# Block three first in the mixer's output, woven TensorE work ahead of its row pair, a third norm buffer

## The reference

```python
x = x + g1 * (mixed @ w_out)                 # the mixer's output
h = modulate(rms_norm(x, norm2_g), sh2, sc2)
q = (h @ w_query).reshape(B, T, 8, 2, 128)   # peer_ffn
s = einsum('bthpd,hpkd->bthpk', q, sub_keys)
s_top, i_top = top_k(s, 16)                  # then top 16 of the 16 x 16 pair sums
idx, gate = chosen experts, softmax(best_s)  # 128 of each for a token
act = gelu(einsum('td,ted->te', h, down[idx]))
y = einsum('te,ted->td', act * gate, up[idx])
# two layers on x and ctx: pooling mixer, then attention; each followed by
x = x + g2 * (silu(a) * v) @ w_down          # a, v from a depthwise conv of h @ w_up
```

## Time and profile before

| | us |
|---|---|
| median of 3 runs | 3761.59 (3760.1 to 3765.12) |
| the profiled execution | 3768.46 |
| its span | 3766.4 |

### The profile page before, as it was taken

The page is one execution under the profiler, slowest core; times in us unless marked ns, Lnnn a source line. Parts: engine busy times, 40 slices in busy tenths (PEclk is TensorE's granted clock), DMA queues, the critical chain, the costliest instruction groups (busy, mean ns, idle before and its releaser), DMA issues.

```text
span 3766.4 us, 59546 instructions
## 1 busy us (share of the span) xinstructions
PE 3306.8 (88%) x24177; PEld 1947.6 (52%) x24177; DVE 2408.0 (64%) x4781; ACT 1114.4 (30%) x2905; POOL 1014.9 (27%) x1021
## 2 busy tenths in 40 slices
PE   7998899899998876666567999999999998999998
PEld 4556666788876332222122333333368854468853
DVE  3865635687756766588777787764444147457765
ACT  2442212444422332333334344332222023410000
POOL 1024410345420333333342233323200000034432
PEclk8999999999999999777788999999999999999999
DMA  4147630000024999999999999989834421012233
GB/s 184 45 184 264 226 113 23 2 11 3 3 86 145 383 414 417 415 405 415 403 414 373 357 389 375 375 344 388 333 108 145 132 74 43 1 68 90 90 123 145
DMA packets 146412, 800.88 MB, mean 213 GB/s; under 512 B 13934, under 2 KB 33773, under 8 KB 62812
## 3 DMA queue, kind: packets, MB, share of 16 engines
q0 software_dynamic: 76048, 543.64, 36.1%
q1 hardware_dynamic: 68940, 251.34, 18.3%
q10 hardware_dynamic: 1152, 2.10, 0.1%
HBM read 794.92 MB, written 2.10 MB: 212 GB/s over the span
## 4 chain that ended last, share of the span: by engine, by line
PE 54%; DVE 13%; DMA 10%; ACT 4%; issue 2%; POOL 0%; DVEq 0%; POOLq 0%; ACTq 0%
PE bank L104 19%; PE bank L2721 8%; DMA row<-in_experts,idxs 7%; PE bank L3154 7%; PE bank L3170 4%; PE bank L4244 3%; DVE row L2914 3%; DMA wring<-in_experts,idxs 2%; PE bank L3946 2%; PE bank L2668 1%; PE bank L1108 1%; DVE wring L2914 1%; PE bank L1089 1%; PE bank L1880 1%; ACT cf L2811 1%
## 5 line engine op out<-in xcount | busy, mean ns | idle before, releaser
L2721 PE MATMUL bank<-row,dg 64*64 64x512 f32 x2920 | 431.8, 703 | 212.2 <-ACT dg L2817 211.8
L2914 DVE CUSTOM_DVE_ANT_0 row<-row,bank 128x1024 f32<-128x1024 f32 x365 | 445.6, 1221 | 192.4 <-DMA row<-in_experts,idxs 154.7
L2981 POOL DMA_INDIRECT row<-in_experts,idxs x365 | 362.3, 993 | 712.7 <-PE bank L2721 643.5
L2721 PEld LDWEIGHTS bank<-row,dg 64*64 64x64 f32 x2920 | 114.9, 148 | 470.6 <-issue 470.0
L3154 PE MATMUL bank<-s_hid,wring 128*128 128x512 f32 x704 | 327.3, 610 | 0.0
L104 PE MATMUL bank<-hT,wring 128*128 128x256 f32 (+1 forms) x864 | 286.6, 492 | 3.0 <-ACT sq L898 3.0
L2808 ACT ACTIVATE act<-dots 128x2 f32<-128x2 f32 x256 | 51.8, 203 | 710.6 <-DVE dots L2914 710.2
L2721 PE MATMUL bank<-wring,dg 64*64 64x512 f32 x1176 | 180.1, 708 | 91.0 <-ACT dg L2817 90.9
L2981 POOL DMA_INDIRECT wring<-in_experts,idxs x147 | 141.7, 964 | 368.7 <-PE bank L2721 264.3
L3154 PEld LDWEIGHTS bank<-s_hid,wring 128*128 128x128 f32 x704 | 129.0, 192 | 200.1 <-issue 199.3
L2914 DVE CUSTOM_DVE_ANT_0 wring<-wring,bank 128x1024 f32<-128x1024 f32 x147 | 179.5, 1221 | 81.0 <-DMA wring<-in_experts,idxs 67.5
(11 more groups left out here) (731 smaller groups left out, 6376.5 us busy)
## 6 DMA issues: line engine op xcount, KB each, us to landing
wring<-in_ffn_up SPq DMA_DIRECT2D x66, 1024.0 KB, 6.8
wring<-in_ada_w SPq DMA_DIRECT2D x64, 1024.0 KB, 6.6
wring<-in_ffn_down SPq DMA_DIRECT2D x32, 704.0 KB, 4.3
wring<-in_ffn_w_down SPq DMA_DIRECT2D x20, 1024.0 KB, 6.5
wring<-in_w_in SPq DMA_DIRECT2D x7, 2048.0 KB, 8.2
wring<-in_peer_w_query SPq DMA_DIRECT2D x8, 1024.0 KB, 25.6
wring<-in_attn_w_qkv SPq DMA_DIRECT2D x3, 2048.0 KB, 7.8
row<-in_experts,idxs POOLq DMA_INDIRECT x365, 9.9
```

Source lines behind the costliest of these rows:

```text
L2721: ins = pe.e.matmul(self.ks[t][64 * half:64 * half + 64, :], self.dg[u % 4][p, 0:64], row[p, 1024 + half * 512:1536 + half * 512], start=( ...
L2914: e.tensor_tensor_reduce(row, row, P.pairs[0], 1.0, 0.0, MUL, ADD, self.dots[:, g % 2, x:x + 1]).then_inc(*V.up("pg_dot", j))
L2981: e.indirect_dma_start(self.places[r], None, P.i["experts"], bass.IndirectOffsetOnAxis(ap=idu[:, b, j % 128:j % 128 + 1], axis=0)).then_in ...
```

## The change

- `MixerOut`: on PE, only block 3's first half is transposed at first; the gates of blocks 2 and 1 come ahead of the output products; an output product is cut in two parts of four matmuls (`part` 0 reads only the delta-rule half), and both first parts of block 3 run before both second parts. Ahead of block 3's row transposes stands only the first part of one product of block 2 (before, both whole products). The other outputs follow after the scores. On DVE the mean step of the norm becomes a function of its own, and two additions of block 2 move behind the first eight steps of `choose`. ACT is ordered to match.
- `Experts`: the query tiles 0 to 7 get four places instead of two (a spent part of the constants, and the scan's `y`), and another order of loads. The fourth gather waits for tile 7 instead of tile 6.
- `Experts.pe`: the woven work of steps u-1 and u runs ahead of the row products of the pair.
- `n10` gets three buffers; only unit 1 stands ahead of the transposes, and turn u-2 follows unit u.
- The loads of the rotation table and of the gains stay at the start of `Qkv`'s stage; the diff doesn't change them.

```diff
-        self.n10 = HiddenState(self, 1, 0, "ffn0", "n10", "ffn0_down_x", 0, [5, 2, 3, 4])
+        self.n10 = HiddenState(self, 1, 0, "ffn0", "n10", "ffn0_down_x", 0, [5, 2, 3, 4], 3)
...
+        self.mean(dv, 3)
         self.normed(dv, 3)
         self.heads_dv(dv, 0)
+        choice, f = P.experts.choose(dv, 3, 0), self.first
+        for _ in range(8):
+            next(choice)
         self.added(dv, 2, 0)
+        next(choice)
         self.added(dv, 2, 1)
-        choice, f = P.experts.choose(dv, 3, 0), self.first
-        for _ in range(11):
+        for _ in range(2):
             next(choice)
         self.added(dv, 1, f)
...
+        self.mean(dv, 2)
         self.added(dv, 1, 1 - f)
         self.added(dv, 0, 1 - f)
-        for b in (2, 1, 0):
+        self.normed(dv, 2)
+        for b in (1, 0):
+            self.mean(dv, b)
+        for b in (1, 0):
             self.normed(dv, b)
...
         x = P.experts
-        for b in self.BLOCKS:
-            self.turned_ac(ac, b, 0)
-        self.root_ac(ac, 2)
+        self.turned_ac(ac, 3, 0)
         ac.wait_ge(*P.at("ro_bonus", 0))
         self.turned_ac(ac, 3, 1)
+        self.root_ac(ac, 2)
         self.root_ac(ac, 1)
+        for b in (2, 1, 0):
+            self.turned_ac(ac, b, 0)
         self.turned_ac(ac, 2, 1)
+        self.squares(ac, 3)
+        self.root(ac, 3)
         for q in range(4):
...
         self.gate_pe(pe, 3)
-        for b in self.BLOCKS:
-            self.turn_pe(pe, b, 0, P.ogdn[:, b])
+        self.turn_pe(pe, 3, 0, P.ogdn[:, 3])
         self.gate_pe(pe, 2)
+        self.gate_pe(pe, 1)
...
         self.heads_pe(pe, 3)
-        self.out_pe(pe, ws, 3, 0)
-        self.out_pe(pe, ws, 3, 1)
-        self.gate_pe(pe, 1)
+        for part in range(2):
+            for half in range(2):
+                self.out_pe(pe, ws, 3, half, part)
+        P.cycle((6, 7, 0, 3, 6, 7, 0, 6, 3, 7, 1))
+        for b in (2, 1, 0):
+            self.turn_pe(pe, b, 0, P.ogdn[:, b])
         self.heads_pe(pe, 2)
...
-        self.out_pe(pe, ws, 2, 0)
         self.heads_pe(pe, 1)
         self.gate_pe(pe, 0)
-        self.out_pe(pe, ws, 2, 1)
+        self.out_pe(pe, ws, 2, 0, 0)
         P.cycle((2, 3, 4, 5))
         self.rows_pe(pe, 3)
...
-        self.out_pe(pe, ws, 1, f)
-        self.out_pe(pe, ws, 0, f)
+        self.out_pe(pe, ws, 2, 0, 1)
+        for b, half in ((2, 1), (1, f), (0, f)):
+            for part in range(2):
+                self.out_pe(pe, ws, b, half, part)
         T_.mark("wfree", ws[f][0])
...
-        self.wq = Tiles(P, "query_w", quarter[2:4] + [first[0], P.mem("wq", 2048)], 8)
+        self.wq = Tiles(P, "query_w", quarter[2:4] + [first[0], P.mem("wq", 2048), P.cst[:, P.idle:P.idle + 2048],
+                                                      P.rout.rs.y.rearrange("p b h i -> p (b h i)")], 8)
...
-        return 2 + n % 2 if n < 8 else n % 2
+        return (2, 3, 4, 2, 3, 4, 5, 2)[n] if n < 8 else n % 2
...
-        for n in range(16):
-            after = None if n < 2 or n in (8, 9) else n - 2
+        for n in (2, 0, 1, 3, 4, 5, 7, 6, 8, 9, 10, 11, 12, 13, 14, 15):
+            after = {3: 0, 4: 1, 5: 2, 7: 3}.get(n) if n < 10 else n - 2
             if n == 0:
                 sy.wait_ge(*P.at("pq_keys", 3))
             if n == 1:
                 sy.wait_ge(*P.at("ro_T", 0, 0))
+            if n == 6:
+                sy.wait_ge(*P.at("ro_T", 0, 1))
...
-            if x % 2 == 0:
-                self.row_pe(pe, u)
-                self.row_pe(pe, u + 1)
             for _ in range(self.steps(u)):
                 next(rest, 0)
...
             P.around.pe(pe, u)
+            if x % 2:
+                self.row_pe(pe, u - 1)
+                self.row_pe(pe, u)
...
-                po.wait_ge(*P.at("query_w_free", 6))
+                po.wait_ge(*P.at("query_w_free", 7))
...
-        return self.tmps[n % 2], self.order[n - 2] if n >= 2 else None
+        return self.tmps[n % self.spare], self.order[n - self.spare] if n >= self.spare else None
...
-        P.cycle((1, 2, 3))
-        for u in range(1, P.qkv.ahead):
-            P.qkv.unit_pe(pe, u)
-        P.cycle((5, 6, 7, 4))
+        P.cycle((1,))
+        P.qkv.unit_pe(pe, 1)
+        P.cycle((5, 6, 7, 2, 3, 4))
         for b in (2, 3, 4):
             P.n10.turn_pe(pe, b)
...
-        self.P.cycle((4, 5, 6, 7, 0, 1, 2, 3))
-        turned = 0
-        for u in range(self.ahead, 14):
+        self.P.cycle((5, 6, 7, 2, 3, 4, 0, 1))
+        for u in range(2, 14):
             self.unit_pe(pe, u)
-            for _ in range(2 if u == self.ahead + 2 else 1):
-                self.turn(pe, turned)
-                turned += 1
-        for u in range(turned, 14):
+            self.turn(pe, u - 2)
+        for u in (12, 13):
             self.turn(pe, u)
```

More of the change, by code:

```diff
@@ L2333, in added, with mean @@
         e.tensor_tensor(P.x[:, b, cs], P.x[:, b, cs], tp, ADD).then_inc(*V.up("x1", half, b))
+    def mean(self, dv, b):
+        st = self.st[:, 56 + 4 * b:60 + 4 * b]
+        dv.wait_ge(*self.P.at("pq_sq", b))
+        dv.e.tensor_scalar(st[:, 1:2], st[:, 0:1], 1.0 / D, 1e-6, MUL, ADD).then_inc(*self.V.up("pq_mean", b))
     def normed(self, dv, b):
@@ L2371, in ac @@
             e.activation(self.skT[:, 4 * q:4 * q + 4, :], v4(P.ps("pq_keys", q)), ACT.Copy).then_inc(*A.up("free", "pq_keys", q))
-        self.squares(ac, 3)
-        self.root(ac, 3)
         self.turned_ac(ac, 1, 1)
+        self.out_ac(ac, 3)
         self.root_ac(ac, 0)
-        self.out_ac(ac, 3)
-        ac.wait_ge(*P.at("ro_y", 0))
         for n in range(8):
             x.query_ac(ac, 0, n)
+            if n == 1:
+                ac.wait_ge(*P.at("ro_y", 0))
             if n:
                 x.scores_ac(ac, 0, n - 1)
-            if n == 3:
-                self.squares(ac, 2)
         self.turned_ac(ac, 0, 1)
@@ L2387, in ac @@
         x.weigh(ac, 3, 0)
+        self.squares(ac, 2)
+        self.root(ac, 2)
         for n in range(8, 16):
@@ L2391, in ac @@
                 x.scores_ac(ac, 0, n - 1)
+            if n == 8:
+                self.squares(ac, 1)
             if n == 9:
-                self.squares(ac, 1)
-            if n == 10:
                 self.squares(ac, 0)
-                self.root(ac, 2)
-            if n == 12:
                 self.root(ac, 1)
-            if n == 14:
                 self.root(ac, 0)
@@ L2474, in pe @@
                 x.scores_pe(pe, 0, n - 1)
-        P.cycle((6, 7, 0, 1))
+        P.cycle((6, 7, 0, 1, 0, 1))
         self.heads_pe(pe, 0)
@@ L2478, in pe @@
         x.scores_pe(pe, 0, 7, k)
-        self.out_pe(pe, ws, 1, f)
-        self.out_pe(pe, ws, 0, f)
+        self.out_pe(pe, ws, 2, 0, 1)
+        for b, half in ((2, 1), (1, f), (0, f)):
+            for part in range(2):
+                self.out_pe(pe, ws, b, half, part)
         T_.mark("wfree", ws[f][0])
-        self.out_pe(pe, ws, 1, 1 - f)
-        self.out_pe(pe, ws, 0, 1 - f)
+        for b, half in ((1, 1 - f), (0, 1 - f)):
+            for part in range(2):
+                self.out_pe(pe, ws, b, half, part)
         T_.mark("wfree", ws[1 - f][0])
@@ L2509, in heads_pe, with out_pe @@
         self.turn_pe(pe, b, 1, self.rs.y[:, b].rearrange("p h i -> p (h i)"))
-    def out_pe(self, pe, ws, b, half):
+    def out_pe(self, pe, ws, b, half, part):
         P = self.P
         w, wb = ws[half]
-        k = P.bank(pe, "ro_o", half, b)
+        k = P.ps("ro_o", half, b) if part else P.bank(pe, "ro_o", half, b)
         pe.wait_ge(*P.at("wload", w))
-        pe.wait_ge(*P.at("free", "ro_T", b, 1))
-        mm(pe.e, k, [(self.oT[c // 4][:, c % 4, b * 128:(b + 1) * 128], wb[:, c, :]) for c in range(8)]).then_inc(*self.T.up("ro_o", half, b))
+        pe.wait_ge(*P.at("free", "ro_T", b, part))
+        ins = mm(pe.e, k, [(self.oT[part][:, c, b * 128:(b + 1) * 128], wb[:, 4 * part + c, :]) for c in range(4)], start=(part == 0), stop=(part == 1))
+        if part:
+            ins.then_inc(*self.T.up("ro_o", half, b))
     def rows_pe(self, pe, b):
@@ L3520, with __init__ @@
 class HiddenState(Stage):
-    def __init__(self, P, layer, which, before, name, made, shift=0, order=None):
+    def __init__(self, P, layer, which, before, name, made, shift=0, order=None, spare=2):
         super().__init__(P, name, before)
@@ L3527, in __init__ @@
         self.As = P.mem("As", 8)
-        self.tmps, self.st = [P.mem("tmp", 1024) for _ in range(2)], P.mem("st", 24)
-        self.order = order
+        self.tmps, self.st = [P.mem("tmp", 1024) for _ in range(spare)], P.mem("st", 24)
+        self.order, self.spare = order, spare
     def rows(self, b):
@@ L4500, in __init__ @@
         self.units = [(2, 0), (2, 1), (2, 5), (0, 5), (2, 2), (2, 3), (2, 4), (0, 2), (0, 3), (0, 4), (1, 5), (1, 2), (1, 3), (1, 4)]
-        self.ahead, self.w = 4, {}
+        self.w = {}
     def sy(self, sy):
```

2 lines of the change are left out of this document (removed).

## The result

The changed kernel took **3703.68 us** (median of 4 runs, 3694.94 to 3710.09) against 3761.97 (4 runs beside it): ratio 0.9843, 95% interval 0.9821 to 0.9864, 58.3 us faster. In a later group of runs it took 3697.55 (5 runs) against 3764.55: 0.9828 (0.9815 to 0.9841). The prediction was 3718 with 3699 to 3744: the direction and the range held, and the gain was 44 where 58 were measured. The profiled execution took 3710.09, its span is 3708.2.

A forecast was written before the change was run, and what follows sets the result against it. During the gathers DMA bounds first, then TensorE, from 2037 to 2719. Parts 1 to 4 sum as 14 + 25 - 3 + 8 = 44 us, giving a median of 3718 from 3761.59, range 3699 to 3744.

The forecast's parts named there:

- part 2: Woven work ahead of the row products: TensorE's large waits for ScalarE's diagonal go, 25 us gained, bounds 10 and 36.
- Part 1: Mixer's output and query tiles: first row product 14 us sooner, bounds 9 and 17; first gather 9 to 10 sooner.
- (a): Mixer's output: VectorE's 5.00 us wait for a gate matmul goes; it adds block 3's output 4.9 us sooner.
- (b): Mixer's output: only half a product ahead of the row transposes; first query product at 1141.0, 10.5 us sooner.
- (c): First eight query products and their scores: 16.4 us instead of 21.2, ending at 1157.4.
- (d): First top-16 to the indices: ready at 1191.5, with a wait of about 2.4 us; first gather 9 to 10 sooner.
- (e): TensorE's remaining output products take 37.8 us, to 1195.9; last queries end at 1212.5, first row product at 1221.5.
- Part 3: Border after the last row pair: its products come 4 us later, TensorE idles before pooling; 3 us lost, 0 to 5.
- Part 4: Norm before the attention, third buffer and query-unit order: VectorE trails by one unit; 8 us gained, 5 to 10.
- DMA did not take ScalarE's place: Rival on the expert rows: DMA cannot bring a pair in 5.94 us, part 2 gives 5, time 3738; chance 0.17.
- The slower one: Rival in the DMA-bound stretch: row products come behind woven work, places come free later, time 3779; chance 0.05.
- The head start: Rival: head start melts, row products start 5 us sooner, not 14, and norm part gives 5; 3730; chance 0.12.

## Why the prediction was right or wrong

The mechanisms were right in the main, and the size of part 2 was not. That the range held is in part luck: by its stages the change gains 66 us, 22 more than predicted, and the first comparison showed 58.3. In the later group the median fell 1.5 below the range. The sentence "the forecast's own range by the bounds is 3700 to 3738" is also off: the bounds of the four parts give gains of 19 to 63, so 3743 to 3699.

**Part 1** (14 predicted, with the first gather 9 to 10): right, a little low. TensorE and VectorE in the changed kernel's mixer's output, where the stage begins 6.4 us later than in the kernel before; take that off:
```profile
1147.43 3.84 PE L2689 MATMUL bank<-hq,row 128*128 128x128 f32 x32 [0.74 <-ACT hq L2439]
...
1164.24 37.93 PE L104 MATMUL bank<-wring,oT 128*128 128x512 f32 x88
1202.01 3.73 PE L2689 MATMUL bank<-hq,wq 128*128 128x128 f32 x32
...
1225.88 1.95 PE L2742 MATMUL bank<-wring,dg 64*64 64x512 f32 x16
```
```profile
1134.23 0.69 DVE L2329 TENSOR_TENSOR y<-y,bank 128x512 f32<-128x512 f32 x1
...
1174.75 0.69 DVE L2338 TENSOR_TENSOR tmp<-bank,gt 128x512 f32<-128x512 f32 x1 [2.60 <-PE bank L104]
...
1198.05 0.20 DVE L2923 CAST idxs<-ia 128x64 uint32<-128x64 f32 x1
```
(a) The wait of 5.00 is gone, and the normed rows came 4.7 sooner (4.9 said). (b) The first query product stands at 1141.0 by the old start (1141.0 said), with no wait for a tile. (c) The end of the first eight, 1157.8 (1157.4). (d) The indices, 1191.8 (1191.5), with the wait of 2.60 that was put at 2.4. (e) Outputs of 37.93 us (37.8), last queries from 1195.6 (1195.9), the first row product at 1219.4 (1221.5), 15.9 sooner. That is 2.1 better than said: the row product follows the woven block with no wait. The step "DMA is full from then on, so the 14 carry on" held but for a little: 16.5 at the first dot product and 16.8 at dot product 256 in this trace, 15.1 and 13.5 in the second one.

**Part 2** (25 predicted, bounds 10 and 36; 47.2 measured): right in its mechanism, wrong in its size, and above its own upper bound. Four terms, by the waits in both traces:
- "eight of 2.4 to 3.5 make 24": they are gone, 24.
- the ten small waits, 9.6 us, of which 2.8 are left: 6.8 more. The step that failed is "some stalls come back as late rows". I had worked out 641 us for TensorE and 628 for DMA and then took something off for their nearness, with no row for it. From dot product 296 to 511 the changed kernel took 641.7.
- "over the stretch this is about 10 us more" of clock stood in the text and was left out of the 25. It was 12.1.
- the three waits at the stretch's start, from 2004 to 2030, were 12.6 and became 8.4: 4.2 that were never looked at, since the view began at 2030.

24 + 6.8 + 12.1 + 4.2 = 47.1. About 4 of the 12.1 can be the execution's own, as said. The bound of 36 was called "all waits and most of the clock", which by its own numbers is 33.6 and 10. A discount belongs in the rival that names its mechanism, and that rival had its 0.17 already. Wrong too was the reading of the releaser: all 33.6 us were taken for ScalarE's, and 11.5 of them follow a dot product that VectorE finished late. The order cures the other kind as well, since it gives VectorE's queue the same cover.

The sign that I had named against it did appear. The waits of VectorE for rows, changed kernel, 2030 to 2670:
```profile
DVE row L2935 <- DMA row<-in_experts,idxs: 81.2, 51, 3.5
...
PE bank L2742 <- ACT dg L2838: 2.8, 3, 1.2
```
VectorE's waits for rows grew from 33.8 to 81.2 us, more than TensorE's fell, and cost nothing that shows: TensorE was busy for 649.1 of the 660.3 us. As a sign it was badly chosen: an engine with slack waits more when the engine that it feeds waits less.

On the price of a switch: without its two table loads the chain of the stall at 2119 shrank from 5.10 to 2.24 us, by 2.86. Two loads as the trace has them are 2.56. By the Trainium skill, page ScalarE: Activation LUTs, section "What ACT_TABLE_LOAD costs", two switches with their drains are an estimated 5.3, more than the whole change of this chain; the trace disagrees, and the measurement decides.

**Part 3** (3 lost predicted, 0 to 5): 5.8 lost, and 1.6 behind it, so it lies outside its bounds. From the last dot product to the last row products it took 2.9 us longer, and the chain behind them came as much later. But the pause of 4.08 did not lie ahead of the pooling products. It lay ahead of a turned block of the fill (L3206), whose eviction (L3354) stands on ScalarE behind the square root of the same chain; the fill behind that turn (3.62 instead of 1.88) and the modulation row (1.78 instead of 1.04) then ran at the lower clock, still ahead of the pooling products. The step "the slack was 1.1" counted the chain's last instruction and not the fill that also waits for the chain; that eviction's slack was 0.1 (it ended at 2730.67, and TensorE went on at 2730.76).

The 1.6 behind it are not the chain's. Later in that stretch both traces of the changed kernel have the same pause of TensorE (1.73 and 1.74 us, for VectorE). Behind it, in this trace, the products that follow ran at the lower level (granted clock 0.86 from 2728 to 2740); in the second trace the clock stayed at 1.00, and the stretch was as short as in the kernel before. What makes one execution fall and the other not, no run here shows.

**Part 4** (8 predicted, 5 to 10): right, 8.3, and 8.4 alone. The last turn of the changed kernel:
```profile
3079.69 1.06 PE L4545 MATMUL bank<-consts,rb 128*128 128x128 f32 x8
3087.42 1.09 PE L4545 MATMUL bank<-consts,rb 128*128 128x128 f32 x4 [6.67 <-DVE rb L4637]
```
One wait of 6.67 where 6 to 7 were named, in place of the 5.25 and 5.83 of the earlier trace rows.

**Rivals.** DMA did not take ScalarE's place: it stands at 1.00 and the rows still come. The slower one is out by the kernel woven from row 288 on. The head start was 3 us smaller at dot product 288 when that part stood alone, within what executions differ by, and did not shrink in the changed kernel. That the change doesn't do what it says is out with the 47.2 and the 8.3.

## What to carry to other kernels

Where an engine weaves two streams and one stream's step needs a chain through other engines that begins at the other stream's step, count the work that lies between the two in program order. If it is shorter than the chain, move the dependent step one block later. Here 5.7 us of cover for a chain of 5.1 gave all that 7.7 gave, and at the end of the loop the distance cost 7 us, so turn the order back for the last step. Price a stall at its idle time and the slow instructions behind it, and before you put a wait down to the engine that the profile names, ask what that engine had waited for.

## What was not expected of the hardware

- Two table loads of 1.28 us around each Silu cost 19.7 us over the kernel where little work stood ahead of the row products, and nothing that can be told where the row pair came a block later.
- After a pause of about 3 us TensorE's next instructions took up to twice as long (3.69 for 1.95; 3.62 for 1.88 after the pause of 4.08). Over the stretch that added some 8 to 12 us to 35.1 of idle time. After a pause of 1.7 us the same instructions slowed in one execution and not in another.
- The same code took 1108.9 us in one trace and 1097.9 in another up to the mixer's output, more than many edits bring. Within one group on one chip it still varied from 1097.9 to 1106.8 over four traces. Windows of the changed kernel in the two executions, first the slower one:
```profile
0.00:100.00 100.00, 75.39 (x325) 51.59 (x326) 32.56 (x103) 27.34 (x60) 10.66 (x24) 0.83 0.46 173
1000.00:1100.00 100.00, 96.13 (x1929) 85.75 (x1919) 62.94 (x104) 29.24 (x67) 27.84 (x29) 0.93 0.01 3
```
```profile
0.00:100.00 100.00, 77.24 (x339) 50.28 (x340) 36.50 (x119) 29.04 (x63) 10.68 (x24) 0.88 0.47 173
1000.00:1100.00 100.00, 95.28 (x1923) 85.55 (x1923) 63.26 (x104) 31.23 (x71) 29.95 (x32) 1.00 0.02 4
```
The granted clock differs, 0.83 and 0.88, 0.93 and 1.00. What sets it from one execution to the next no run here shows. An edit of some 8 us is read from distances within a stage, not from the medians.
